# Panels of the next feed-forward block in places of their own, and the sums of squares behind the last product, at three boundaries of a two-block transformer kernel

## The reference

```python
y = <mixer output> @ w_out
x = x + g * rmsnorm(y, norm_g[l, 1])
h = modulate(rmsnorm(x, norm_g[l, 2]), sh2, sc2)
y = sqrelu_mlp(h, mlp_w1[l], mlp_w2[l])        # first product of the feed-forward: h @ w1
```

## Time and profile before

| | us |
|---|---|
| median of 3 runs | 2169.81 (2168.37 to 2170.53) |
| the profiled execution | 2171.98 |
| its span in the trace | 2169.9 |
| PE busy in it | 2094.8 (97%) |
| POOL / DVE / ACT busy | 968.0 / 1119.1 / 885.0 |

### The profile page before, as it was taken

One profiled execution on the slowest core, in us unless ns is written; L12 is line 12 of the kernel. 1 busy time (PEld: TensorE's weight loads), 2 busy tenths in 40 slices (PEclk: granted clock), 3 DMA queues, 4 the chain that ended last, 5 costly groups with the idle time before them and its releaser, 6 DMA issues.

```text
span 2169.9 us, 28079 instructions
## 1 busy us (share of the span) xinstructions
PE 2094.8 (97%) x9946; PEld 1702.7 (78%) x9946; DVE 1119.1 (52%) x1749; ACT 885.0 (41%) x1506; POOL 968.0 (45%) x489
## 2 busy tenths in 40 slices
PE   8999999989999999999999999999999999999997
PEld 5777787778888888787768888888777788888887
DVE  3534743334677776763473543434575435343435
ACT  4225874445222222434474422323465544323233
POOL 3436776343454444334123344444435623444443
PEclk9998999999999999999999999999999999999999
DMA  4440053204366664364102233333222012333332
GB/s 179 165 142 5 21 195 94 76 15 157 124 229 229 220 224 162 97 230 148 30 1 83 78 97 97 97 97 97 78 88 68 1 59 69 97 97 97 97 97 88
DMA packets 67925, 234.47 MB, mean 108 GB/s; under 512 B 7296, under 2 KB 10752, under 8 KB 67712
## 3 DMA queue, kind: packets, MB, share of 16 engines
q1 hardware_dynamic: 67840, 233.33, 33.1%
HBM read 231.20 MB, written 2.10 MB: 108 GB/s over the span
## 4 chain that ended last, share of the span: by engine, by line
PE 60%; issue 21%; POOL 9%; DVE 5%; ACT 4%; DMA 1%; POOLq 0%; SPq 0%; DVEq 0%; ACTq 0%
PE bank L892 18%; PE bank L893 17%; PE bank L894 17%; POOL WL L756 6%; PE bank L988 1%; PE bank L1111 1%; PE bank L1003 1%; DMA stage<-panels 1%; POOL sq L810 1%; PE bank L1176 0%; DVE acc L2286 0%; ACT WH L1581 0%; PE bank L1478 0%; POOL t L810 0%; PE bank L1210 0%
## 5 line engine op out<-in xcount | busy, mean ns | idle before, releaser
L756 POOL TENSOR_TENSOR WL<-stage,WH 128x1024 fp32r<-128x1024 f32 x264 | 657.2, 2491 | 943.3 <-ACT WH L1581 943.1
L1581 ACT ACTIVATE WH<-stage 128x1024 fp32r<-128x1024 f32 x264 | 279.8, 1060 | 828.5 <-PE bank L894 779.4
L892 PE MATMUL bank<-H,WH 128*128 128x512 f32 (+1 forms) x1324 | 510.2, 385 | 24.2 <-POOL WL L756 11.6
L893 PE MATMUL bank<-H,WH 128*128 128x512 f32 (+1 forms) x1324 | 507.8, 384 | 0.0
L894 PE MATMUL bank<-H,WL 128*128 128x512 f32 (+1 forms) x1324 | 507.3, 383 | 0.0
L892 PEld LDWEIGHTS bank<-H,WH 128*128 128x128 f32 x1324 | 250.6, 189 | 79.4 <-issue 21.5
L894 PEld LDWEIGHTS bank<-H,WL 128*128 128x128 f32 x1324 | 250.7, 189 | 48.8
L893 PEld LDWEIGHTS bank<-H,WH 128*128 128x128 f32 x1324 | 250.7, 189 | 48.0 <-issue 0.5
L2628 DVE TENSOR_TENSOR Y<-bank,Y 128x512 f32<-128x512 f32 x328 | 215.7, 684 | 94.8 <-PE bank L894 94.1
L892 PE MATMUL bank<-HID,WH 128*128 128x512 f32 (+1 forms) x688 | 264.3, 384 | 0.1
L893 PE MATMUL bank<-HID,WH 128*128 128x512 f32 (+1 forms) x688 | 264.2, 384 | 0.0
(11 more groups left out here) (435 smaller groups left out, 3365.9 us busy)
## 6 DMA issues: line engine op xcount, KB each, us to landing
stage<-panels SPq DMA_DIRECT2D x296, 512.0 KB, 3.7
ahead<-ada SPq DMA_DIRECT2D x96, 512.0 KB, 5.3
RAW<-panels SPq DMA_DIRECT2D x18, 512.0 KB, 4.4
apiece<-ada SPq DMA_DIRECT2D x16, 512.0 KB, 3.7
x<-xT SPq DMA_DIRECT2D x3, 1024.0 KB, 8.5
outT<-x SPq DMA_DIRECT2D x16, 128.0 KB, 1.7
x<-xT SPq DMA_DIRECT2D x2, 512.0 KB, 4.6
Y<-bias SPq DMA_DIRECT2D x1, 1024.0 KB, 6.0
```

The source lines that it names most:

```text
L756: pool.tensor_tensor(low_of(p, slot), stage[:, slot, :], high_of(p, slot).bitcast(F32), ALU.subtract).then_inc(s_split, 1)
L892: pe.matmul(out, wh, rh, start=start, stop=False)
L893: pe.matmul(out, wh, rl, start=False, stop=False)
L1581: act.activation(high_of(p, slot), stage[:, slot, :], ACT.Copy).then_inc(s_hisplit, 1)
```

## The change

- Two new tables of places. `IN_WC`: c2 and c3 of `a_out` go to `WC`, which lies over queries and keys of the cells. `IN_WY`: q0 and q1 of all three feed-forwards go to `WY`. `WD` moves away from there, to the space of the values (units 104 to 120).
- SP: c2 and c3 of `a_out` are loaded before the wait for the last head. In the first feed-forward the adaptive weights (`ahead`) share space with `WY`, so the first four of them are loaded only once PE has used q1, by a wait on SP.
- ACT: the copies of q0 and q1 move forward, behind the evacuations of c6 and c7 (first half); those of q2 and q3 also move to before the last evacuation; one of them stands ahead of the evacuation of c6 (second half). The copy of c2 of `a_out` runs in the cells, that of c3 right behind them. `extra_high` is gone from the three boundaries.
- POOL: all of c2 to q3 are split before the residual; c2 and c3 of `a_out` right behind `cells()`.
- PE: the sums of the squares of x go to bank `G[1]`, with no warming matmuls and no wait for the logarithm ahead of them.

```diff
+IN_WC = {PANEL0["a_out"] + 2: 0, PANEL0["a_out"] + 3: 1}
+IN_WY = {PANEL0[_name] + _j: _j for _name, _, _ in FFNS for _j in range(2)}
...
-        WD = place(72, "WD", [P, 2, 2, D], F32R)
+        WC = place(72, "WC", [P, 2, 2, D], F32R)
+        WD = place(104, "WD", [P, 2, 2, D], F32R)
...
-            plain(p0, p0 + 4)
-            for k in range(4):
-                load_ahead(AHEAD0 + k, k)
-            plain(p0 + 4, p0 + 6)
-            for k in range(4, 8):
+            plain(p0, p0 + 6)
+            for k in range(4, 8):
+                load_ahead(AHEAD0 + k, k)
+            sp.wait_ge(s_used, p0 + 2)
+            for k in range(4):
                 load_ahead(AHEAD0 + k, k)
...
-            plain(PANEL0["a_out"], PANEL0["a_out"] + 2)
+            plain(PANEL0["a_out"], PANEL0["a_out"] + 4)
             sp.wait_ge(cell["split"], HEADS - 1)
             sp.wait_ge(cell["last_split"], 1)
...
-                for p in range(p0 + 2, p0 + 8):
-                    split_low(p, p % 2)
-                boundary(name, p0 + 8)
+                for p in range(p0 + (4 if name == "a" else 2), p0 + 12):
+                    split_low(p, p % 2)
                 residual(name)
...
+                for p in (PANEL0["a_out"] + 2, PANEL0["a_out"] + 3):
+                    split_low(p, p % 2)
...
                 half_sums(name, 1)
-                warm(G[1], 8)
-                pe.wait_ge(s_log, upto(LOG, name, 1))
                 for half in range(2):
                     for m in range(KC):
-                        pe.matmul(ST[:, COLS[half]], ones, Y[:, m, COLS[half]], ...)
-                warm(G[1], 14)
+                        sum_after(half, m)        # the same matmul into G[1]
+                warm(AD, 14)
...
                 for c in range(4, KC):
                     both(0, c, T[c % 2][:, COLS[0]])
-                    if c == 4:
-                        panel_high(p0 + 7, 1)
+                    if c != 5:
+                        panel_high(p0 + (7, None, 8, 9)[c - 4], (1, None, 0, 1)[c - 4])
                 half_root(name, 0)
                 second(4)
+                panel_high(p0 + 10, 0)
...
                 square_after(name, 0, 4)
+                panel_high(p0 + 11, 1)
                 second(6)
-                panel_high(p0 + 8, 0)
                 square_after(name, 0, 5)
                 square_after(name, 0, 6)
                 second(7)
                 half_root(name, 1)
                 square_after(name, 0, 7)
-                panel_high(p0 + 9, 1)
...
+                if s == steps + 2:
+                    panel_high(PANEL0["a_out"] + 2, 0)
                 if kb == 3 and n >= 2:
                     cell_high(n - 2)
+            panel_high(PANEL0["a_out"] + 3, 1)
```

More of the change, by code:

```diff
@@ L399, in high_of @@
         def high_of(p, slot):
+            if isinstance(p, int) and p in IN_WC:
+                return WC[:, IN_WC[p], 0, :]
+            if isinstance(p, int) and p in IN_WY:
+                return WY[:, IN_WY[p], 0, :]
             if isinstance(p, int) and p in IN_WD:
@@ L414, in low_of @@
         def low_of(p, slot):
+            if isinstance(p, int) and p in IN_WC:
+                return WC[:, IN_WC[p], 1, :]
+            if isinstance(p, int) and p in IN_WY:
+                return WY[:, IN_WY[p], 1, :]
             if isinstance(p, int) and p in IN_WD:
@@ L739, in _ @@
             sp.dma_start(apiece[:].bitcast(I32)[:, 0, 0:S], pos).then_inc(s_pos, 16)
-            plain(PANEL0["a_out"] + 2, NPANEL)
+            plain(PANEL0["a_out"] + 4, NPANEL)
             for m in range(KC):
@@ L776, in residual, with after_projection @@
                     pool.tensor_tensor(x[:, m, cols], x[:, m, cols], Y[:, m, cols], ALU.add).then_inc(s_resp, 1)
-            def boundary(name, p0):
-                split_low(p0, 0)
+            def after_projection(name, p0):
+                for p in range(p0 + (4 if name == "a" else 2), p0 + 12):
+                    split_low(p, p % 2)
                 residual(name)
-                split_low(p0 + 1, 1)
-            def after_projection(name, p0):
-                for p in range(p0 + 2, p0 + 8):
-                    split_low(p, p % 2)
-                boundary(name, p0 + 8)
             def after_feed_forward(name, p0):
@@ L859, in _ @@
             after_projection("ca", PANEL0["mem_o"])
-            split_extra("ffn")
             split_lows(PANEL0["ffn"] + 4, PANEL0["a_in"] + 2)
@@ L866, in _ @@
             after_projection("a", PANEL0["a_out"])
-            split_extra("mlp0")
             split_lows(PANEL0["mlp0"] + 4, PANEL0["kv_a"] + 2)
@@ L881, in _ @@
             after_projection("b", PANEL0["b_out"])
-            split_extra("mlp1")
             after_feed_forward("mlp1", PANEL0["mlp1"])
@@ L917, in pair_of @@
                         slot = (p + j) % 2
-                        last = three(banks[j][:, :], WH[:, slot, k * P:(k + 1) * P], WL[:, slot, k * P:(k + 1) * P],
+                        last = three(banks[j][:, :], high_of(p + j, slot)[:, k * P:(k + 1) * P],
+                                     low_of(p + j, slot)[:, k * P:(k + 1) * P],
                                      H[:, k, 0, :], H[:, k, 1, :], k == 0, k == KC - 1)
@@ L1025, in sums_after, with sum_after @@
                 after = HALVED[name][1]
+                def sum_after(half, m):
+                    pe.wait_ge(s_sq, upto(SQ, after, half, m))
+                    pe.matmul(G[1][:, COLS[half]], ones, Y[:, m, COLS[half]], start=m == 0, stop=m == KC - 1)\
+                        .then_inc(s_sum, 1)
                 half_sums(name, 1)
-                warm(G[1], 8)
-                pe.wait_ge(s_log, upto(LOG, name, 1))
                 for half in range(2):
                     for m in range(KC):
-                        pe.wait_ge(s_sq, upto(SQ, after, half, m))
-                        pe.matmul(ST[:, COLS[half]], ones, Y[:, m, COLS[half]], start=m == 0, stop=m == KC - 1)\
-                            .then_inc(s_sum, 1)
-                warm(G[1], 14)
+                        sum_after(half, m)
+                warm(AD, 14)
             def last_chunks(name):
@@ L1687, in root_after @@
                 act.wait_ge(s_sum, upto(SUM, after, 1, KC - 1))
-                act.activation(logs[:, :], ST[:, :], ACT.Ln, bias=eps[:, :], scale=1.0 / D).then_inc(s_log, 1)
+                act.activation(logs[:, :], G[1][:, :], ACT.Ln, bias=eps[:, :], scale=1.0 / D).then_inc(s_log, 1)
                 act.wait_ge(s_log, upto(LOG, after, None))
@@ L1707, in evacuate_halves @@
                 for c in range(4):
-                    if c < 2:
+                    if c < 2 and name != "a":
                         used(p0 + c, c)
@@ L2064, in _ @@
             evacuate_halves("ca")
-            extra_high("ffn", 0)
             root_after("ca")
-            extra_high("ffn", 1)
             high("x_ffn", scaled_in, hh, lambda m: col("zero"))
@@ L2259, in _ @@
             evacuate_halves("b")
-            extra_high("mlp1", 0)
             root_after("b")
-            extra_high("mlp1", 1)
             high("x_mlp1", scaled_in, hh, lambda m: adac[:, (LAYER1 + SH2) * 8 + m:(LAYER1 + SH2) * 8 + m + 1])
```

2 lines of the change are left out of this document (removed).

## The result

The changed kernel took 2155.97 us in the median of 4 runs (2153.95 to 2163.01), the kernel before 2170.17 in 4 (2168.37 to 2172.56): ratio 0.994, interval 0.9915 to 0.9964. Timed twice more, on two other occasions beside the kernel before, it had ratios of 0.9951 (0.9932 to 0.997) and 0.9949 (0.9931 to 0.9966). So it is 0.5 to 0.6% faster, some 11 to 14 us. (One execution of the kernel before, of 7051.68 us, is in a slow state and is left out everywhere.)

The account below looks back on a forecast made before the run. TensorE, busy 97% of the span, was taken as the bound. 3 x (1.7 + 1.0) + 2.7 = 10.8 us off 2169.81 gave 2159.0, range 2155.8 to 2163.5.

Parts of the forecast that it names:

- Sums, 1.7 at each boundary: At each boundary, sums of squares without 8 warming matmuls end at 526.4, not 528.09: 1.7 us, bounds 1.0 and 2.0.
- They meet: In the sums, PE alone ends at 526.07, the last square's sum at 526.08 earliest: at most 2.0 us saved.
- q3's copy ahead of c6, 0.2 late: Before c6's second-half evacuation, q3's copy makes c7 and the squares 0.2 us late, between 0 and 0.95.
- Copies gone from behind the last evacuation, 1.0: At each boundary, without q3's copy in front, chunk 0 is rounded at 530.36, not 531.35: 1.0 us, bounds 0.8 and 1.1.
- the remark that the earlier sums need this move: At each boundary, q2's copy hid under ACT's 1.54 us wait for sums, so moving it is needed for the 1.7.
- `a_out`, 2.7: At the start of `a_out`, PE's waits before c2 and c6 shrink by 2.7 us, bounds 2.2 and 3.6.
- The exclusion of VectorE and GpSimd: Before `a_out`, POOL's c2 split holds the shared port first, so DVE's last-head product and the angles come 2.3 us later.
- SP's wait and `ahead`, nothing: In the first feed-forward, panel 7's load is held up some 5 us and costs nothing; it would show from 10.
- A: Rival: `a_out` gives more and the late evacuation costs nothing, 12.6 us, so 2157.2; chance 0.17.
- B: Rival: q3's copy shows whole and c6 of `a_out` waits for its ring, 7.2 us, so 2162.6; chance 0.17.
- C: Rival: late feed-forward panels take up the earlier start, gain under 4.3 us; chance 0.03.
- D: Rival: without the 8 matmuls the clock falls in the sums, 17.7 us slower, so 2187.5; chance 0.03.

Follow-up runs that it names:

- sums_only: Kernel before with only the sums of squares of x sent to `G[1]`, no 8 warming matmuls, no logarithm wait; 2169.92 us against 2167.26, ratio 1.0016.
- q3_last: Kernel before with the new sums and q3's copy moved behind the rounding of the eight chunks; 2160.50 us against 2168.12, ratio 0.9958.
- last_head_first: Changed kernel with GpSimd waiting for VectorE's last-head product before splitting c2 of `a_out`; 2160.78 us in one run, kernel before 2168.12.
- panels_only: Changed kernel with the old sums (`ST`, 8 matmuls, wait) back and without the `a_out` part; 2165.95 us against 2167.26 before, ratio 0.9996.

## Why the prediction was right, point by point

*The time.* 2159.0 was forecast, 2155.97 measured: inside the range by 0.2 us only, which is partly luck, and outside the 2157.5 to 2161 that had 0.60. The sum was 10.8; the traces show 9.8, the runs at one clock 9.8 and 11.3. The first medians differ by 14.2, and the later ones by 10.7 and 12.9: what lies above the traces' 9.8 is not found in any edge, and I put it down to the spread of executions, which isn't shown. So the sum was about 1 us too high, and the absolute time came out lower than forecast without the change giving more.

*Sums, 1.7 at each boundary: mis-sized.* Measured 1.45, 1.50 and 1.10. The step that failed is "They meet". I let the sums start at 519.00 by the record of the first warming matmul, 1.11 us behind the start of the last product, and run for 7.07 us. In the changed kernel they start 0.53 us behind the start of line 1028's record (the half sum with c7's square), which is 1.44 us behind the last product, and they took 7.31. With c7 on time (sums_only) it is 1.30 and 7.31, so 0.4 us of the 2.02 isn't there to gain. PE is still the late one: the last square is done at 526.20, its sum could end at 526.64, the logarithm starts at 527.09. The sign I had named, a logarithm within 0.6 us of the last square, did not come: it is 0.89. That the 8 matmuls were what delayed it is shown by sums_only: 1.6 us to the logarithm.

*q3's copy ahead of c6, 0.2 late: right in place.* The chain is as written: c6 at 516.77 (forecast 516.3, with c6 itself 0.4 us later in that trace), VectorE's last additions from 518.02 (516.62 before), x6's square at 518.46, c7 right behind. The delay of c7 is 0.17 and 0.12 us at "ca" and "a" of the first trace, and at "b" 0.52 and 0.62 in two traces, where the load of q2 came late, and 0.12 in the third, where it did not. With the copy behind c6 the evacuation of c7 is on time, 0.32 us behind the last product, at all three. q2 itself was copied at 511.36, where 511.0 was forecast.

*Copies gone from behind the last evacuation, 1.0: right.* From the logarithm to the rounding 2.25 us instead of 3.2. And the remark that the earlier sums need this move was the weightiest of all: alone, the sums gave nothing (0 of 1.6 each). But I put the need at q2's copy. It was q3's: its load hangs on the split of q1, which the earlier sums don't move. q3_last leaves q2's copy where it was and loses nothing.

*`a_out`, 2.7: near the measured 3.0, by two errors that cancel; that is luck.* I took all of the 2.90 at c2; 0.59 stayed, the evacuation of c0 that c2's bank needs. And I had 0.5 to 1.5 us left at c6; none was. The angles were ready when forecast (1154.35, where c0 starts 0.7 us earlier than before, so 1155.05 on the prediction's axis, for 1155.2). But ACT loaded the table of the sine at 1152.29 while it still waited for them, so the sine ran right behind them, at 1154.38, and c4's copy at 1157.18 (1157.9 on that axis), not 1159.1.

*The exclusion of VectorE and GpSimd.* The product took 2.80 us, and POOL came first (1141.64 against 1141.79), as written. By the rule of the Trainium skill ("SBUF — State Buffer", section "SBUF: two separate sides"), that whichever starts first holds the ports for its whole instruction, the trace agrees here and in last_head_first, where the order was turned and the next instruction paid.

*SP's wait and `ahead`, nothing: right.* From the feed-forward's first product to c0 of `a_out` it is 607.1, 605.7 and 605.2 us in three traces, against 605.8 before; the longest has a stretch of low clock at 1035 us.

*Rivals.* A and B: neither; the boundaries lie between the two. C didn't occur. D: the clock is 1.00 through the sums and the products behind them (519 to 535 us). Its mechanism was real in another kernel: sums_only lost the clock at all three boundaries, where PE stood 3 us, but behind the sums, and it cost 1.8 us at "b" (364.8 us from there to the end, 363.0 before) and not 9.5. The windows have length, busy time of PE, PEld, DVE, ACT and POOL, clock, DMA share and GB/s.

```profile
519.00:530.00 11.00, 10.81 (x49) 8.77 (x48) 6.29 (x15) 6.84 (x17) 2.54 (x4) 1.00 0.65 238
530.00:535.00 5.00, 4.32 (x20) 3.38 (x19) 4.94 (x8) 2.75 (x5) 0.00 (x0) 1.00 0.00 0
```

## What to carry to other kernels

A wait that two engines run into in turn is paid once: taking 1.6 us out of the first (the sums) gave nothing until the second (a copy that waits for its load, in front of the first rounding) was out of the way as well. So before moving many things early, move the one instruction that stands in front of the critical one to behind it; at these boundaries that did what new places and a new order did. And with a gain near the spread of executions, compare edges in traces, or times at one clock on the same occasion, and ask first whether the edit itself moves the clock.

## What the runs showed of the hardware that I had not expected

- TensorE's granted clock fell behind stretches in which it did nothing. At the boundaries and at c2 of `a_out` it was 0.66 to 0.67 over the next 5 us behind all ten stretches of 2.98 to 3.33 us, and 1.00 behind the three of 2.90 us (before, panels_only, sums_only) and behind all of 0.68 to 1.65 us. But the length alone doesn't decide: near 427 us PE waits 2.36 us in every one of the fourteen traces, and the clock fell right behind it in nine and stayed at 1.00 in five.
- ScalarE's load of an activation table ran while the activation that needs it still waited for its operand: 1.28 us from 1152.29, with the angles ready only at 1154.35.
- One kernel's executions on one occasion differ by 7 to 13 us, and most of it goes with the mean granted clock (1.65 us for each 0.001).
